# Where the last head pair's bonus step and its state store stand in a list of steps

## The chip, the cores and the metric

The kernel runs on one core of one Trainium2 chip. The metric is the device time of one execution in microseconds (us). The engines are TensorE (PE in the profile; its weight loads are PEld), VectorE (DVE), ScalarE (ACT), GpSimd (POOL) and SyncE (SP), which here only issues DMAs. Every engine works through its own instructions in order, and the engines hold each other by semaphores.

## The reference, cut to what matters

One layer of a hybrid model for 128 context tokens and 512 latent tokens, 1024 channels. Three branches read one input projection: an RWKV-7 scan of 8 heads of 64 channels in both directions, a gated MLP and a convolution. Their concatenation goes through one output projection; a mixture of 16 experts (top 2) follows. The part that the change touches is the scan branch:

```python
def step(s, inp):
    r_t, w_t, k_t, v_t, kk_t, a_t = inp
    s_kk = jnp.einsum('bhvk,bhk->bhv', s, kk_t)
    s = (s * w_t[:, :, None, :]
         - s_kk[..., None] * (kk_t * a_t)[:, :, None, :]
         + v_t[..., None] * k_t[:, :, None, :])
    return s, jnp.einsum('bhvk,bhk->bhv', s, r_t)
...
y = _head_norm(ys[0] + ys[1], lp['lnx_g'], lp['lnx_b'])
bonus = jnp.sum(heads(r) * heads(kts[0] + kts[1]) * lp['r_k'], axis=-1, keepdims=True) * heads(v)
ya = ((y + bonus.reshape(B, T, D_A)) * g).astype(h.dtype)
```

The kernel returns the outputs of both token groups and the scan's final context states (`new_state_rwkv`).

## The kernel before, in words

The work is done in stages: the modulation, the norm and the input projection with the gated MLP and the convolution; the scan; the output projection with the second norm and the router; the experts; the final norm. All five engines go from the scan to the output projection through `scan_done` (L1178), a list of semaphore waits on everything that the scan produced, among them `state_stored` (the state stores have landed) and `read_head_bonus` (the last head bonus is multiplied).

**The scan** works on four head pairs m = 0 to 3 (two heads, 128 partitions each). A pair's set-up is low_rank, decay, key_square, key_norm, mix, kk, factors and operands; `gram`, `keys`, `xloc`, `wqx`, `mr` work on one of five groups q of chunks (64 tokens each, both directions); diag, sub 1-30, turn, off, merge_a and merge_b invert the chunks' triangular matrices; `chain m s` carries the state through slot s (order 2, 0, 3, 1, 4 to 8; slots 0 and 1 are the context, so the final context state is there after `chain m 1`); `y m t` gives the output of one of five token tiles; `state_out` transposes the final context state, copies it and stores it; the head steps (head_stats, head_centre, head_scale, head_gain, head_bias, head_bonus) normalise the pair's output and add the bonus.

**The order is written out by hand.** `PLAN` (L338) is one text list of steps. `steps_of` turns it into `SCHEDULE`, and each of the engines walks the same list in its own function (`scan_loads` L498 for SyncE, `scan_pool` L536, `scan_act` L565, `scan_dve` L698, `scan_pe` L827) and issues its part of each step, with its waits. So a step's place in the list is its place in the queue of every engine that has a part in it.

**Shared PSUM.** Steps that write a temporary in PSUM take one of three double banks in turn, in the order of the list: `temp(st)` is `pp[i % 3]` for the i-th such step, and TensorE first waits until the step three places before has been read (`temp_free`, L394). bonus, state_out and head_bonus are among these steps; chain has its own banks.

**bonus m** has four parts: GpSimd adds the keys of both directions (L562, `kt_sum`), VectorE multiplies by r_k and r (L748, `bonus_terms`), TensorE sums over each head with five narrow matmuls (L864, `bonus_mm`), ScalarE copies the result (L619, `read_bonus`), which head_bonus reads. **state_out m**: four transposes on TensorE (L878) once `state_next (m, 1)` is up, a copy on ScalarE (L688) once the previous pair's store has landed, two DMAs of SyncE to the output (L532). **head_bonus m**: five transposes on TensorE (L883), a multiply (L491) and an add (L496) on VectorE.

**The early loads.** At the step `chain 3 2` SyncE reads back the two other branches into `catBC` and issues the loads for the next stage (`early_loads`, L1135: four DMAs, two of w_out and the two token groups). They overwrite buffers of the scan, so SyncE first waits for what still uses these:

```python
if st == ("chain", 3, 2):

    sp.wait_ge(*at("y_mm", (2, TILES_Y[-1])))
    sp.wait_ge(*at("keys_T", (3, STAGES[-1])))
    for n in ("factor", "end_factor", "operands_done", "bonus_mm", "excl", "kt_sum", "mb_mm", "read_merge_a", "wb_diag"):
        sp.wait_ge(*at(n))
    sp.wait_ge(*at("cat_moved", "stored"))
    sp.dma_start(catBC[:, :, :].rearrange("p c t -> p (c t)"), cat_dram).then_inc(*up16("cat_moved", "back"))
    early_loads(sp)
```

A name without a key stands for the semaphore's last count, that is all four pairs. SyncE's next step in the list is `state_out 3`, and behind that it goes on to the next stage (`post_loads`, L1184): the rest of w_out, the modulation rows, the norm's gain and the router's weights.

**Behind the scan** (`post_pe`, L1626, in the order of `ORDER`): TensorE's first work are the head matmuls (L1655, the gate), then the output projection's matmuls (L1647); VectorE's first is the gate's product (L1388).

Of the kernel before, what the change touches and what calls it, by code (L numbers as in the profile page):

```python
# [40 lines left out]
def build(nc, A, outs, counts):  # L41
# [25 lines left out]
    with ctx:  # L67
        counts.open(nc, ctx)

        def sb(name, shape, dt=F32):  # L70
            return ctx.enter_context(nc.sbuf_tensor(name, shape, dt))
# [219 lines left out]
        def ccols(c):  # L291
# [39 lines left out]
        bonus = sb("bonus", [P, NT, NH])  # L331
# [23 lines left out]
            keys 1 3 / sub 2 13 / mr 1 0 / wqx 1 2 / sub 2 14-15 / low_rank 3 1 1 / sub 2 16-17 / keys 1 4 / chain 1 0 / mr 1 2 /  # L355
            chain 1 3 / sub 2 18-19 / xloc 1 3 / chain 1 1 / wqx 1 3 / sub 2 20-22 / key_square 3 1 / chain 1 4 / xloc 1 4 / mr 1 3 /
            key_norm 3 0 / chain 1 5 / sub 2 23 / decay 3 1 / sub 2 24 / wqx 1 4 / state_out 1 / sub 2 25 / chain 1 6 / key_norm 3 1 /
            sub 2 26 / y 1 0 / mix 3 / mr 1 4 / sub 2 27 / chain 1 7 / sub 2 28 / factors 3 0 / head_scale 0 / sub 2 29 / y 1 2 /
            sub 2 30 / chain 1 8 / y 1 3 / turn 2 / off 2 / kk 3 0 / y 1 1 / factors 3 1 / kk 3 1 / operands 3 0 / merge_a 2 / y 1 4 /
            merge_b 2 / operands 3 1 / head_gain 0 / gram 2 1 / gram 2 0 / head_bias 0 / diag 3 / sub 3 1-3 / keys 2 1 / keys 2 0 /  # L360
            xloc 2 1 / head_bonus 0 / sub 3 4 / xloc 2 0 / gram 2 2 / gram 2 3 / wqx 2 1 / sub 3 5-6 / keys 2 2 / mr 2 1 / head_stats 1 /
            wqx 2 0 / init 2 / keys 2 3 / sub 3 7 / xloc 2 2 / sub 3 8 / chain 2 2 / xloc 2 3 / sub 3 9 / mr 2 0 / sub 3 10 / gram 2 4 /
            wqx 2 2 / chain 2 0 / chain 2 3 / sub 3 11-12 / mr 2 2 / keys 2 4 / chain 2 1 / sub 3 13-16 / wqx 2 3 / chain 2 4 / xloc 2 4 /
            mr 2 3 / wqx 2 4 / sub 3 17 / chain 2 5 / y 2 0 / sub 3 18-19 / chain 2 6 / sub 3 20 / mr 2 4 / sub 3 21 / chain 2 7 / y 2 2 /
            sub 3 22 / chain 2 8 / sub 3 23-25 / y 2 3 / sub 3 26 / y 2 1 / sub 3 27-28 / y 2 4 / sub 3 29 / state_out 2 / sub 3 30 /
            gram 3 1 / gram 3 0 / turn 3 / head_centre 1 / head_scale 1 / keys 3 1 / keys 3 0 / xloc 3 1 / off 3 / head_gain 1 / init 3 /
            gram 3 2 / merge_a 3 / head_bias 1 / head_bonus 1 / merge_b 3 / head_stats 2 / xloc 3 0 / gram 3 3 / wqx 3 1 / keys 3 2 /
            mr 3 1 / wqx 3 0 / xloc 3 2 / head_centre 2 / gram 3 4 / head_scale 2 / mr 3 0 / chain 3 2 / wqx 3 2 / keys 3 3 / chain 3 0 /
            keys 3 4 / xloc 3 3 / chain 3 3 / mr 3 2 / head_gain 2 / chain 3 1 / wqx 3 3 / chain 3 4 / y 3 0 / mr 3 3 / chain 3 5 /
            xloc 3 4 / head_bias 2 / chain 3 6 / wqx 3 4 / chain 3 7 / y 3 2 / mr 3 4 / y 3 3 / chain 3 8 / head_bonus 2 / y 3 1 / y 3 4 /  # L370
            bonus 3 / head_stats 3 / head_centre 3 / head_scale 3 / head_gain 3 / state_out 3 / head_bias 3 / head_bonus 3
        """


# [1850 lines left out]
```

## Time and profile before

| | |
|---|---|
| device time, median of 3 runs | 1016.51 us (1015.21 to 1020.67) |
| the profiled execution | 1015.5 us |
| its span | 1013.8 us, granted TensorE clock 0.876 on the mean |
| busy: PE, PEld | 795.3 us (78%), 494.0 us (49%) |
| busy: DVE, ACT, POOL | 499.8 us (49%), 264.2 us (26%), 127.9 us (13%) |
| moved by DMA | 150.58 MB |

The page gives shares over the whole span, which are means over stages with different limits. A stage is read from the timeline of each engine (what ran when, and in brackets how long the engine had been idle and what ended that) and from the list of waits. Busy times of TensorE rest on modelled ends of its matmuls.

### The profile page before, as it was taken

How to read it: one execution, taken by the hardware profiler on the slowest of the kernel's cores; microseconds unless marked ns; L12 is line 12 of the kernel's file. 1: busy time of each engine (PE TensorE's matmuls, PEld its weight loads, DVE VectorE, ACT ScalarE, POOL GpSimd, SP SyncE). 2: the span in 40 equal slices, each digit the busy share in tenths (PEclk: the TensorE clock that was granted, in tenths of full speed). 3: DMA queues.
4: the chain of work that ended last, by engine and by line, in shares of the span. 5: the costliest groups of instructions: out<-in, count | busy, mean ns of one | idle time of the engine just before them, and what ended most of it. 6: DMA issues, size and time to landing. Idle time of an engine off the chain costs nothing. (4 is left out here: it accounts for less than half of the span.)

```text
span 1013.8 us, 18006 instructions
## 1 busy us (share of the span) xinstructions
PE 795.3 (78%) x7510; PEld 494.0 (49%) x7510; DVE 499.8 (49%) x1052; ACT 264.2 (26%) x561; POOL 127.9 (13%) x127
## 2 busy tenths in 40 slices
PE   4589999999933719979699957998279999999800
PEld 3345455655522507767577743455244454444400
DVE  1210037575455898989999650533613333333302
ACT  2221013121246435646644610102010010000003
POOL 3000000000004130310300000000032222222050
PEclk9679999999966858979799978998569999999955
DMA  7952044064061000000000058101079999999476
GB/s 281 340 203 81 2 167 166 4 246 167 1 231 51 2 1 3 22 10 3 8 3 9 4 193 321 43 21 62 18 280 374 354 356 365 356 370 350 141 149 184
DMA packets 42442, 150.58 MB, mean 149 GB/s; under 512 B 6031, under 2 KB 8598, under 8 KB 37398
## 3 DMA queue, kind: packets, MB, share of 16 engines
q1 hardware_dynamic: 33142, 78.07, 21.4%
q0 software_dynamic: 9216, 71.31, 20.7%
q8 instruction: 62, 1.02, 0.4%
q14 instruction: 22, 0.18, 0.1%
HBM read 133.08 MB, written 22.05 MB: 153 GB/s over the span
## 5 line engine op out<-in xcount | busy, mean ns | idle before, releaser
L2167 PE MATMUL banks<-arena 128*128 128x512 f32 x304 | 157.4, 600 | 0.0
L1714 PE MATMUL banks<-arena 128*128 128x512 f32 x288 | 129.2, 602 | 1.1 <-ACT arena L1343 1.1
L2166 PEld LDWEIGHTS banks<-arena 128*128 128x128 f32 x304 | 57.9, 193 | 73.4 <-issue 71.5
L1714 PEld LDWEIGHTS banks<-arena 128*128 128x128 f32 x288 | 55.5, 193 | 71.1 <-issue 69.5
L1737 PE MATMUL banks<-arena 128*128 128x512 f32 x144 | 65.1, 595 | 1.6 <-DVEq L1160 1.6
L1586 DVE TENSOR_TENSOR arena<-arena,banks 128x256 f32<-128x256 f32 x18 | 7.6, 420 | 111.4 <-ACT arena L1349 105.5
L2046 DVE TENSOR_TENSOR arena<-arena 128x641 f32<-128x641 f32 x15 | 12.4, 827 | 99.6 <-ACT arena L1911 99.6
L2166 PE MATMUL banks<-arena 128*128 128x128 f32 x304 | 59.9, 279 | 1.5 <-ACT arena L201 1.5
L775 DVE TENSOR_TENSOR arena<-arena 128x30 f32<-128x30 f32 (+14 forms) x120 | 52.3, 436 | 4.1
L1349 ACT ACTIVATE arena<-banks 128x256 f32<-128x256 f32 x18 | 6.9, 385 | 180.5 <-PE banks L1714 180.5
L2036 DVE SCALAR_TENSOR_TENSOR arena<-arena 128x640 f32<-128x640 f32 x60 | 49.7, 878 | 0.0
L772 DVE TENSOR_TENSOR arena<-arena 128x30 f32<-128x30 f32 (+14 forms) x120 | 45.7, 381 | 2.7
L2167 PEld LDWEIGHTS banks<-arena 128*128 128x128 f32 x304 | 46.7, 194 | 0.0
L1260 POOL DMA_INDIRECT arena<-in_moe_w_gu_dram,loraT x18 | 17.1, 951 | 196.2 <-DVE arena L1553 115.4
L1601 DVE SCALAR_TENSOR_TENSOR arena<-banks,loraT,arena 128x512 f32<-128x512 f32 x36 | 25.4, 746 | 32.6 <-PE banks L1737 32.6
L1737 PEld LDWEIGHTS banks<-arena 128*128 128x128 f32 x144 | 26.1, 191 | 28.6 <-issue 25.8
L541 POOL MEMSET arena<- 128x2560 f32 x1 | 2.2, 2231 | 290.1 <-ACT catBC L211 290.1
L1647 PE MATMUL banks<-arena,catBC 128*128 128x512 f32 x80 | 36.3, 607 | 0.3 <-DVE rkvT L1398 0.3
L1647 PE MATMUL banks<-arena,rkvT 128*128 128x512 f32 x80 | 35.3, 593 | 0.0
L2150 PE MATMUL banks<-arena 128*128 128x512 f32 x80 | 34.5, 592 | 0.0
L1908 ACT ACTIVATE arena<-banks 128x128 f32<-128x128 f32 x15 | 4.2, 279 | 105.4 <-PE banks L2167 105.4
L259 PE MATMUL banks<-arena 128*2 128x128 f32 x768 | 26.5, 297 | 3.6 <-DMA arena<-in_ada_w_dram 3.6
(345 smaller groups left out, 1473.8 us busy)
## 6 DMA issues: line engine op xcount, KB each, us to landing
arena<-in_ada_w_dram SPq DMA_DIRECT2D x12, 2048.0 KB, 12.5
arena<-in_w_in_dram SPq DMA_DIRECT2D x5, 2048.0 KB, 14.9
slot_rows<-arena SPq DMA_DIRECT2D x18, 512.0 KB, 8.6
arena<-modulations SPq DMA_DIRECT2D x8, 512.0 KB, 8.2
h_rows<-arena SPq DMA_DIRECT2D x5, 512.0 KB, 2.6
out_dram<-arena SPq DMA_DIRECT2D x5, 512.0 KB, 4.1
arena<-in_x_sample_dram SPq DMA_DIRECT2D x4, 512.0 KB, 11.0
arena<-in_w_out_dram SPq DMA_DIRECT2D x1, 2048.0 KB, 10.6
```

What stands on the lines that cost most here:

```text
L259: x = nc.tensor.matmul(out[32 * g:32 * g + 2, :], silu_c[:, k, :], wslot(n)[:, k, g * P:(g + 1) * P], start=False, stop=(k == KD - 1), ski ...
L772: v.tensor_tensor(t, vsub[:, j + 1:32, j:j + 1].to_broadcast([P, n, j]), vsub[:, j:j + 1, 0:j].to_broadcast([P, n, j]), ALU.mult).then_inc ...
L775: v.tensor_tensor(vsub[:, j + 1:32, 0:j], vsub[:, j + 1:32, 0:j], t, ALU.add).then_inc(*up("inverse_step", ("sub_add", m, j)))
L1260: g.indirect_dma_start(wgu[:, s, :, :].rearrange("p k n -> p (k n)"), None, wgu_rows, bass.IndirectOffsetOnAxis(ap=weight_u[:, i:i + 1], a ...
L1601: v.scalar_tensor_tensor(yrow[:, i % 2, cs], ps[5 + hf][:, :], slot_gate[:, i:i + 1], gate_row[:, i % 2, cs], ALU.mult, ALU.mult) \
L1647: x = T_.matmul(ps[6 + hf][:, :], lhs, wout[:, i, hf * 512:(hf + 1) * 512], start=(i == 0), stop=(i == KD - 1))
L1714: x = T_.matmul(ps[2 + s][:, :], hT[:, s, c, :], wgu[:, s, c, :], start=(c == 0), stop=(c == KD - 1))
L1737: x = T_.matmul(ps[5 + hf][:, :], actT[:, s, c * P:(c + 1) * P], wdn[:, s, c, hf * 512:(hf + 1) * 512], start=(c == 0), stop=(c == 1))
L2036: v.scalar_tensor_tensor(dst, src, ccol[:, 2 * k + c:2 * k + c + 1], dst, ALU.mult, ALU.add) \
L2150: x = T_.matmul(ps[2 + t % 2][:, :], h1T[:, k, t * P:(t + 1) * P], wslot(n)[:, k, :], start=(k == 0), stop=(k == KD - 1))
L2166: T_.matmul(ctx_[:, 0:P], w, h1T[:, k, 0:P], start=(k == 0), stop=(k == KD - 1))
L2167: x = T_.matmul(lat[:, :], w, h1T[:, k, P:T], start=(k == 0), stop=(k == KD - 1))
```

## The change

Two steps of the list move. `bonus 3` stood behind `y 3 4`, the last output tile; now it stands behind `keys 3 4`, the last keys. `state_out 3` stood behind `head_gain 3`; now it stands behind `chain 3 8`, the last chain step, ahead of `head_bonus 2`. The rest of the text that differs is only wrapped differently. No instruction is added or taken away. The end of the list, before and after:

```diff
-            mr 3 1 / wqx 3 0 / xloc 3 2 / head_centre 2 / gram 3 4 / head_scale 2 / mr 3 0 / chain 3 2 / wqx 3 2 / keys 3 3 / chain 3 0 /
-            keys 3 4 / xloc 3 3 / chain 3 3 / mr 3 2 / head_gain 2 / chain 3 1 / wqx 3 3 / chain 3 4 / y 3 0 / mr 3 3 / chain 3 5 /
-            xloc 3 4 / head_bias 2 / chain 3 6 / wqx 3 4 / chain 3 7 / y 3 2 / mr 3 4 / y 3 3 / chain 3 8 / head_bonus 2 / y 3 1 / y 3 4 /
-            bonus 3 / head_stats 3 / head_centre 3 / head_scale 3 / head_gain 3 / state_out 3 / head_bias 3 / head_bonus 3
+            wqx 3 0 / xloc 3 2 / head_centre 2 / gram 3 4 / head_scale 2 / mr 3 0 / chain 3 2 / wqx 3 2 / keys 3 3 / chain 3 0 / keys 3 4 /
+            bonus 3 / xloc 3 3 / chain 3 3 / mr 3 2 / head_gain 2 / chain 3 1 / wqx 3 3 / chain 3 4 / y 3 0 / mr 3 3 / chain 3 5 /
+            xloc 3 4 / head_bias 2 / chain 3 6 / wqx 3 4 / chain 3 7 / y 3 2 / mr 3 4 / y 3 3 / chain 3 8 / state_out 3 / head_bonus 2 /
+            y 3 1 / y 3 4 / head_stats 3 / head_centre 3 / head_scale 3 / head_gain 3 / head_bias 3 / head_bonus 3
```

## Rows read from the trace of the kernel before

Times are us from the start of the span. The first group of a view says what its columns are.

**Rows 1.** the page: GB/s in 40 slices of the span

```profile
GB/s 281 340 203 81 2 167 166 4 246 167 1 231 51 2 1 3 22 10 3 8 3 9 4 193 321 43 21 62 18 280 374 354 356 365 356 370 350 141 149 184
```

**Rows 2.** list of waits, 560 to 725: waiter, releaser, us, times, longest

```profile
PE banks L1655 <- DMA out_dram<-arena: 18.1, 1, 18.1
...
POOL loraT L1234 <- DMA out_dram<-arena: 103.1, 1, 103.1
```

**Rows 3.** list of SyncE's own waits, whole span, same columns

```profile
SPq L524 <- PE banks L864: 41.0, 1, 41.0
```

**Rows 4.** timeline of SyncE's issues: start us, us, queue, line, operation

```profile
594.89 0.33 SPq L526 DMA_DIRECT2D catBC<-branches  x1
...
597.49 3.92 SPq L532 DMA_DIRECT2D out_dram<-arena  x2
...
614.13 0.39 SPq L1188 DMA_DIRECT2D arena<-in_w_out_dram  x1
```

**Rows 5.** DMA, 590 to 640: GB/s, 40 slices; an issue, KB, landing us

```profile
GB/s 0 7 13 0 123 205 401 398 416 426 423 406 410 416 416 410 403 381 68 0 82 308 406 423 419 423 416 209 341 298 397 419 416 397 134 3 13 0 0 0
...
out_dram<-arena SPq DMA_DIRECT2D x2, 32.0 KB, 14.7
```

**Rows 6.** the line of the state stores (L532), all eight

```profile
DMA to landing us min/median/max: 2.0/2.3/15.8
```

**Rows 7.** timeline of TensorE, 573 to 600: start us, us, line, operation, count

```profile
577.12 0.68 PE L920 MATMUL banks<-arena 64*64 64x64 f32 x16
...
593.25 1.30 PE L864 MATMUL banks<-head_select,arena 128*128 128x2 f32 x10 [0.58 <-DVE arena L748]
```

**Rows 8.** timeline of TensorE around an earlier bonus and an earlier state_out

```profile
393.79 1.28 PE L864 MATMUL banks<-head_select,arena 128*128 128x2 f32 x10
...
482.36 0.30 PE L878 MATMUL banks<-ident,arena 64*64 64x64 f32 x4
```

**Rows 9.** timeline of VectorE: [idle before, and what ended it]

```profile
578.61 0.29 DVE L823 TENSOR_TENSOR arena<-banks,arena 128x128 f32<-128x128 f32 x1 [2.68 <-PE banks L969]
...
592.23 0.88 DVE L748 SCALAR_TENSOR_TENSOR arena<-arena,param_cols,rkvT 128x640 f32<-128x640 f32 x1
...
598.68 0.82 DVE L491 TENSOR_TENSOR rkvT<-banks,bonus 128x640 f32<-128x640 f32 x1
```

**Rows 10.** timeline of ScalarE, 574 to 598

```profile
578.52 0.36 ACT L635 COPY arena<-banks 128x256 f32<-128x256 f32 x1
...
592.74 0.27 ACT L652 COPY arena<-banks 128x128 f32<-128x128 f32 x1 [0.82 <-PE banks L992]
```

**Rows 11.** windows: length, busy PE, PEld, DVE, ACT, POOL; PEclk, DMA share, GB/s

```profile
575.00:590.00 15.00, 15.00 (x398) 12.96 (x393) 5.92 (x19) 6.62 (x19) 0.00 (x0) 1.00 0.02 4
...
614.00:618.00 4.00, 3.71 (x5) 1.67 (x6) 0.69 (x1) 0.00 (x0) 1.51 (x11) 0.50 0.60 172
```

**Rows 12.** timeline of TensorE behind the scan, 600 to 730

```profile
614.29 2.05 PE L1655 MATMUL banks<-g,loraT 128*128 128x512 f32 x2 [18.13 <-DMA out_dram<-arena]
...
616.13 8.07 PE L1647 MATMUL banks<-arena,catBC 128*128 128x512 f32 x16
...
632.79 1.02 PE L1655 MATMUL banks<-g,loraT 128*128 128x512 f32 x2
...
650.07 7.03 PE L1647 MATMUL banks<-arena,catBC 128*128 128x512 f32 x16
```

**Rows 13.** windows of TensorE alone: busy us, granted clock, DMA share, GB/s

```profile
702.00:704.00 2.00, 0.82 (x6) 0.89 0.00 0
```

**Rows 14.** DMA, 10 to 60 (GB/s, queue q1); TensorE's timeline there

```profile
GB/s 297 382 390 385 388 387 387 385 388 387 388 385 392 379 388 387 387 400 405 381 363 193 194 244 220 205 301 392 388 397 390 398 385 383 387 392 393 377 385 378
...
q1 hardware_dynamic: 9345, 17.99, 103.3%
...
20.69 2.00 PE L259 MATMUL banks<-arena 128*2 128x128 f32 x64
```

**Rows 15.** DMA, 575 to 595, queue of instruction blocks: packets, MB, share

```profile
q8 instruction: 4, 0.07, 1.4%
```

More of the change, by code:

```diff
@@ L357, in build @@
             key_norm 3 0 / chain 1 5 / sub 2 23 / decay 3 1 / sub 2 24 / wqx 1 4 / state_out 1 / sub 2 25 / chain 1 6 / key_norm 3 1 /
-            sub 2 26 / y 1 0 / mix 3 / mr 1 4 / sub 2 27 / chain 1 7 / sub 2 28 / factors 3 0 / head_scale 0 / sub 2 29 / y 1 2 /
-            sub 2 30 / chain 1 8 / y 1 3 / turn 2 / off 2 / kk 3 0 / y 1 1 / factors 3 1 / kk 3 1 / operands 3 0 / merge_a 2 / y 1 4 /
-            merge_b 2 / operands 3 1 / head_gain 0 / gram 2 1 / gram 2 0 / head_bias 0 / diag 3 / sub 3 1-3 / keys 2 1 / keys 2 0 /
@@ L361, in build @@
[L361 to L364, printed above, removed]
@@ L365, in build @@
-            sub 3 22 / chain 2 8 / sub 3 23-25 / y 2 3 / sub 3 26 / y 2 1 / sub 3 27-28 / y 2 4 / sub 3 29 / state_out 2 / sub 3 30 /
-            gram 3 1 / gram 3 0 / turn 3 / head_centre 1 / head_scale 1 / keys 3 1 / keys 3 0 / xloc 3 1 / off 3 / head_gain 1 / init 3 /
-            gram 3 2 / merge_a 3 / head_bias 1 / head_bonus 1 / merge_b 3 / head_stats 2 / xloc 3 0 / gram 3 3 / wqx 3 1 / keys 3 2 /
-            mr 3 1 / wqx 3 0 / xloc 3 2 / head_centre 2 / gram 3 4 / head_scale 2 / mr 3 0 / chain 3 2 / wqx 3 2 / keys 3 3 / chain 3 0 /
@@ L369, in build @@
-            keys 3 4 / xloc 3 3 / chain 3 3 / mr 3 2 / head_gain 2 / chain 3 1 / wqx 3 3 / chain 3 4 / y 3 0 / mr 3 3 / chain 3 5 /
-            xloc 3 4 / head_bias 2 / chain 3 6 / wqx 3 4 / chain 3 7 / y 3 2 / mr 3 4 / y 3 3 / chain 3 8 / head_bonus 2 / y 3 1 / y 3 4 /
-            bonus 3 / head_stats 3 / head_centre 3 / head_scale 3 / head_gain 3 / state_out 3 / head_bias 3 / head_bonus 3
+            sub 2 26 / y 1 0 / mix 3 / mr 1 4 / sub 2 27 / chain 1 7 / sub 2 28 / factors 3 0 / head_scale 0 / sub 2 29 / y 1 2 / sub 2 30 /
@@ new lines, in build @@
+            chain 1 8 / y 1 3 / turn 2 / off 2 / kk 3 0 / y 1 1 / factors 3 1 / kk 3 1 / operands 3 0 / merge_a 2 / y 1 4 / merge_b 2 /
+            operands 3 1 / head_gain 0 / gram 2 1 / gram 2 0 / head_bias 0 / diag 3 / sub 3 1-3 / keys 2 1 / keys 2 0 / xloc 2 1 /
+            head_bonus 0 / sub 3 4 / xloc 2 0 / gram 2 2 / gram 2 3 / wqx 2 1 / sub 3 5-6 / keys 2 2 / mr 2 1 / head_stats 1 / wqx 2 0 /
+            init 2 / keys 2 3 / sub 3 7 / xloc 2 2 / sub 3 8 / chain 2 2 / xloc 2 3 / sub 3 9 / mr 2 0 / sub 3 10 / gram 2 4 / wqx 2 2 /
@@ new lines, in build @@
+            chain 2 0 / chain 2 3 / sub 3 11-12 / mr 2 2 / keys 2 4 / chain 2 1 / sub 3 13-16 / wqx 2 3 / chain 2 4 / xloc 2 4 / mr 2 3 /
+            wqx 2 4 / sub 3 17 / chain 2 5 / y 2 0 / sub 3 18-19 / chain 2 6 / sub 3 20 / mr 2 4 / sub 3 21 / chain 2 7 / y 2 2 / sub 3 22 /
+            chain 2 8 / sub 3 23-25 / y 2 3 / sub 3 26 / y 2 1 / sub 3 27-28 / y 2 4 / sub 3 29 / state_out 2 / sub 3 30 / gram 3 1 /
+            gram 3 0 / turn 3 / head_centre 1 / head_scale 1 / keys 3 1 / keys 3 0 / xloc 3 1 / off 3 / head_gain 1 / init 3 / gram 3 2 /
@@ new lines, in build @@
+            merge_a 3 / head_bias 1 / head_bonus 1 / merge_b 3 / head_stats 2 / xloc 3 0 / gram 3 3 / wqx 3 1 / keys 3 2 / mr 3 1 /
+            wqx 3 0 / xloc 3 2 / head_centre 2 / gram 3 4 / head_scale 2 / mr 3 0 / chain 3 2 / wqx 3 2 / keys 3 3 / chain 3 0 / keys 3 4 /
+            bonus 3 / xloc 3 3 / chain 3 3 / mr 3 2 / head_gain 2 / chain 3 1 / wqx 3 3 / chain 3 4 / y 3 0 / mr 3 3 / chain 3 5 /
+            xloc 3 4 / head_bias 2 / chain 3 6 / wqx 3 4 / chain 3 7 / y 3 2 / mr 3 4 / y 3 3 / chain 3 8 / state_out 3 / head_bonus 2 /
```

## The prediction

> **What bounds the kernel now.** I began with the page: the span is the 1013.8 us of the table above, and the kernel runs through stages one after the other, so what a change in one stage is worth has to be read there. The list of waits over the end of the scan and the start of the stage behind it has one entry that dwarfs the others: TensorE's first matmul behind the scan (L1655) sat 18.1 us until a DMA from the arena to an output, the state store, had landed [rows 2]. Next come SyncE's own waits: at L524 its queue stood 41.0 us until the bonus matmuls (L864) were done [rows 3]. L524 is the first of the five early loads' chain of waits that had not yet come; the wait on `bonus_mm` asks for the count of all four pairs, and the last is pair 3. SyncE's timeline puts it in order [rows 4]: the five loads are issued from 594.89 on, the state store of pair 3 goes out behind them on the same queue from 597.49 on, and 614.13 is when SyncE, held by the same `scan_done`, goes on. The rate of the DMA engines shows what filled the time: fifteen slices of 1.25 us, nearly all of them at 380 to 426 GB/s, some 6.6 MB in all, and the store lands about 14.7 us after its issue [rows 5]. The eight state stores have a median of 2.3 us and a longest of 15.8 us [rows 6]: the last pair alone is slow, and it is the one behind the loads. VectorE finished the scan's work, the head bonus of pair 3, at about 600.4 (the multiply from 598.68 to 599.50, then one add) [rows 9]. So between 600.4 and 614.3 nothing computes; a 64 KB store waits out 6.6 MB of loads, and the loads waited for five narrow matmuls at 593.25 [rows 7].
>
> **What the change does to this, part by part.** *Bonus 3 behind keys 3 4.* What is removed at the tail is a VectorE product (0.88 us), a group of ten TensorE passes (1.30 us) and a ScalarE copy; their removal there frees nothing, because the last `y` copy ends at 593.01 [rows 10], when the product was just ending (592.23 + 0.88) [rows 9], and the head statistics need that copy in any case. What is added: the same three in the middle of the chain. VectorE: 0.88 us in a stretch where it sat 2.68 us for TensorE [rows 9], so nothing. GpSimd's sum for it needs no other step of the chain: GpSimd did nothing for the 103.1 us before 614.3 [rows 2], so it was made by 511; a late sum would hold TensorE's queue and all its chain steps. ScalarE: one short copy between the `keys 3 4` copies, the last of them ending at 578.88 [rows 10], and a copy that waits for TensorE; nothing. TensorE: it was busy in 15.00 of 15.00 us from 575 to 590 [rows 11], the other engines wait for it, so here I charge the step in full: 1.28 us, as another bonus step cost in a dense stretch [rows 8]. Above would be a stall on the way in, below zero by hidden latency; 0 to 2 us.
>
> The shared PSUM buffers rotate by three, so a step put into the list makes the three steps behind it wait for readers one place later in the list. For `xloc 3 3` that is the copy of `keys 3 3`, over before it; for `mr 3 2` that of `keys 3 4`, over at 578.88 [rows 10], while TensorE in its new timing can't reach it before 579.4 (577.12, the bonus at 1.28, `xloc` and `chain`) [rows 7, 8]; the third waits for the bonus copy itself. None adds.
>
> *State_out 3 behind chain 3 8.* Four small transposes, 0.30 us [rows 8], on a TensorE that has no idle time there; charged in full. ScalarE's copy leaves its place behind the head statistics and comes at about 591.5. `y 3 4` now waits for that copy, and can't start before 593 anyhow. The store itself, two DMAs, is issued at about 591.7 instead of 597.49.
>
> *The five loads*, not named in the diff, are what moves. TensorE reaches the bonus at 577.12, where `xloc 3 3` now starts [rows 7]; it ends at 578.40. Before, SyncE issued 0.34 us behind the modelled end (593.25 + 1.30 to 594.89) [rows 4, 7], so now at 578.74. The other waits of that list are for work of pair 3's set-up and for `keys 3 4`, all done by then. From the first load to the landed store it was 614.13 - 594.89 = 19.24 us [rows 4]; the same again gives 597.98 for the state store, if it queues behind all the loads as before.
>
> *The end of the scan.* VectorE's tail comes 1.28 + 0.30 = 1.58 us later: the head bonus multiply, the last thing that `scan_done` wants of VectorE, ends at 599.50 + 1.58 = 601.08. That is 3.1 us later than the store, so the tail now ends last. With the 0.16 us between SyncE's and TensorE's release before [rows 4, 12], TensorE starts again at 601.2 instead of 614.29: **13.1 us** earlier. What follows starts from the same `scan_done` on every engine, with the same queue behind it, and is shifted whole: the first reader of the loads finds them landed, as before.
>
> *The clock.* Behind the pause before, the granted clock was at 0.50, the lower of its two levels (1.2 GHz) [rows 11]: the pair of head matmuls took 2.05 us where a later one took 1.02, the first sixteen of the output projection 8.07 where a later group took 7.03 [rows 12]. Those 2.1 us would be saved if the shorter pause, about 6 us (from the last `y` copy's start, 592.74 + 1.58 [rows 10], and five transposes of the head bonus, to 601.2), kept the clock up. I don't count on it: at 702 to 704, with TensorE busy for only 0.82 of 2 us, the granted clock's mean had already fallen to 0.89 [rows 13]. TensorE: Matmul & The Clock Gate, in the Trainium skill (Why this matters for your kernels), warns of a slower clock after idle gaps between bursts of matmuls; by that rule too the 2.1 us are paid again.
>
> Sum: 1015.5 us for the profiled execution (1013.8 of span and 1.7 around it) less 13.1 gives **1002.4 us**. That execution lies 1.0 below the median of the three runs shown (1016.51), which the same step would take to 1003.4; both lie in what follows.
>
> **The rivals.** *More is gained* (17%): TensorE takes the two moved steps in the shadow of waits that the modelled matmul ends hide (1.58 us), or the clock stays up (2.1 us). Both give 998.7, one alone 1000.3 to 1000.8. For it: the profile's matmul ends are modelled, so that 15.00 of 15.00 may hide short waits. Against: those 15.00 as they stand, and the clock's row.
>
> *The store still ends last* (13%): the loads now run beside the scan's last steps, and if they are slower, the store lands later than 601.1. The 3.1 us of slack are gone when the loads' 15.9 us (6.6 MB at some 415 GB/s) become 19, at 347 GB/s; at the 281 GB/s of the page's first slice [rows 1] they take 23.5 us, the store lands at 605.6 and the time is 1007. Against: 380 to 400 GB/s beside a working TensorE at 10 to 60 us [rows 14].
>
> *The loads are not released* (5%): another wait of SyncE's list, or the place of the loads in the queue, keeps them where they are. Then the store at 591.7 isn't ahead of them, since SyncE's order has the loads first; the pause stays, the moved steps come on top, and the time is 1015 to 1017: no change. Against: the wait that ended last is named, L864 [rows 3].
>
> *Slower than before* (3%): TensorE's instructions come by DMA, through the same engines as the loads; four such blocks came in 575 to 595 [rows 15]. If each stood behind the loads as the state store did (14.7 us instead of 2.3, [rows 5, 6]), 12.4 us each, TensorE would stand still in the scan's last steps. It decides from a total of 13.1 us, that is with two blocks of the four late and not fetched ahead; two are 24.8 us, 1027 us. Against it: at 20.69, with the DMA queue at 103% of the 16 engines' time over 10 to 60, TensorE issued 64 narrow passes in 2.00 us without idling [rows 14]. The Trainium skill has both halves: Runtime: NRT & Kernel Launch (Instruction fetch mechanics) says that instructions are fetched by DMA ahead of use, and DMA: Bandwidth & Descriptors (Queues, rings and completion order) that a DMA engine takes turns between queues packet by packet; by the second, a block would not wait out the loads and this rival would cost almost nothing. No row here shows the turn-taking itself.
>
> **How the numbers follow.** The forecast, with 62%, is 1002.4. The range takes in the larger gain (998.7) and most of the later store, with the 1.0 us to the median: 998.5 to 1006.5. Runs of this kernel can tell about 0.5% from no change, 5.1 us. Below 1011.4 are the forecast, the larger gain and the later store: 92% faster; 5% the same; 3% slower.
>
> **What would show it.** In the profile after, SyncE's loads should be issued at 578 to 580, the state store at 591 to 593, with a landing time of some 5 to 6 us; TensorE's first L1655 should stand at about 601 with an idle time of about 6 us before it, ended by VectorE's head bonus (L491), not by a DMA; `xloc 3 3` and all behind it should stand 1.2 to 1.6 us later, with the same spacing. If the idle time before L1655 is ended by a DMA, the store still ends last; if gaps open in TensorE's scan steps under the loads, they are slowed by them; if the loads start later than 581, I have read the wait wrongly.

## The result and the profile after

The changed kernel takes 1011.99 us (median of 15 runs, 1008.6 to 1014.77), the kernel before beside it 1016.69 us (15 runs, 1014.96 to 1021.18). The ratio, which goes by the means of all runs (1011.7 and 1017.9 us) and not by the medians, is 0.994, 95% interval 0.9923 to 0.9957: 6.1 us less (4.4 to 7.8). The forecast was 1002.4 us, 13.1 us less; the range ended at 1006.5 us. The direction was right, and less than half of the gain came.

The profiled execution of the changed kernel took 1014.77 us, the longest of its fifteen. SyncE's timeline in it, columns as in [rows 4]:

```profile
584.28 0.33 SPq L526 DMA_DIRECT2D catBC<-branches  x1
...
602.14 1.31 SPq L532 DMA_DIRECT2D out_dram<-arena  x2
```

The loads go out 10.6 us earlier than before, and the state store no longer stands behind them. It lands within 2.9 us; the line of the state stores, which answers to [rows 6]:

```profile
DMA to landing us min/median/max: 2.0/2.2/2.9
```

TensorE's list of waits, 560 to 725, columns as in [rows 2]:

```profile
PE banks L1655 <- issue: 7.4, 1, 7.4
PE banks L878 <- issue: 3.2, 1, 3.2
...
PE banks L969 <- issue: 1.3, 1, 1.3
```

The 18.1 us for the store's landing are gone. In their place stand 7.4 us put down to "issue", time in which the profile shows nothing that the engine waited for, and two entries that are not in the list of before at all: 3.2 us at a state_out transpose (L878) and 1.3 us at a chain step (L969). TensorE's timeline shows where, columns as in [rows 7]:

```profile
582.67 1.28 PE L864 MATMUL banks<-head_select,arena 128*128 128x2 f32 x10
...
594.17 0.45 PE L969 MATMUL banks<-arena 64*64 64x64 f32 x8 [1.33 <-issue]
...
597.97 0.30 PE L878 MATMUL banks<-ident,arena 64*64 64x64 f32 x3
...
601.47 0.24 PE L878 MATMUL banks<-ident,arena 64*64 64x64 f32 x1 [3.20 <-issue]
...
602.36 1.18 PE L984 MATMUL banks<-arena 128*64 128x64 f32 x16
603.47 0.71 PE L992 MATMUL banks<-arena 64*64 64x64 f32 x16
604.10 1.17 PE L984 MATMUL banks<-arena 128*64 128x64 f32 x16
...
613.99 2.05 PE L1655 MATMUL banks<-g,loraT 128*128 128x512 f32 x2 [7.43 <-issue]
615.83 8.77 PE L1647 MATMUL banks<-arena,catBC 128*128 128x512 f32 x16
```

The longer wait lies between the third and the fourth of four transposes, and the fourth needs nothing that the third did not. Behind it the `y` steps (L984) take 1.17 us; in the kernel before they took 0.70:

```profile
591.58 0.70 PE L984 MATMUL banks<-arena 128*64 128x64 f32 x16
592.21 0.46 PE L992 MATMUL banks<-arena 64*64 64x64 f32 x16
```

VectorE's head bonus of pair 3 then ends at 612.69, columns as in [rows 9]:

```profile
611.87 0.82 DVE L491 TENSOR_TENSOR rkvT<-banks,bonus 128x640 f32<-128x640 f32 x1
```

**One measure for all runs.** In this execution bonus 3 starts at 582.67, 5.5 us later than `xloc 3 3`, whose place it takes, did in [rows 7]. That difference arose ahead of the moved steps and comes and goes between executions of one kernel (the last section). So from here on I read the stretch from bonus 3's start to the first L1655 (L1654, L1659 or L1660 in kernels with other line numbers), the **restart**. The forecast has 601.2 - 577.12 = 24.1 us for it; the changed kernel has 613.99 - 582.67 = 31.3. Of the missing 7.2 us, 6.1 lie ahead of the end of the multiply (612.69 - 582.67 = 30.0 instead of 601.08 - 577.12 = 24.0) and 1.1 between it and the restart (1.30 instead of 0.16).

### The profile page after: what moved, and what is told of

Same layout as the page of the kernel before. It is cut to its first block and busy times, and to the rows that moved or that the text cites. A ratio compares the mean times of both kernels' runs of the same rounds, so it can differ in the third digit from the quotient of the medians.

```text
span 1013.0 us, 18006 instructions
## 1 busy us (share of the span) xinstructions
PE 801.1 (79%) x7510; PEld 499.7 (49%) x7510; DVE 500.2 (49%) x1052; ACT 264.2 (26%) x561; POOL 128.1 (13%) x127
## 5 line engine op out<-in xcount | busy, mean ns | idle before, releaser
L2046 DVE TENSOR_TENSOR arena<-arena 128x641 f32<-128x641 f32 x15 | 12.4, 827 | 99.6 <-ACT arena L1911 99.6
L802 DVE TENSOR_TENSOR arena<-banks,causal_mask 128x512 f32<-128x512 f32 x40 | 25.4, 683 | 7.8 <-PE banks L896 7.7
```

The source lines that it names most:

```text
L802: v.tensor_tensor(dst, t[:, :, :, w, :], gmask[:, w, :, :, :].rearrange("p i d n -> p (i d) n").unsqueeze(1).to_broadcast([P, 2, 4, 64]), ...
```

## The experiments

**The theories.** *A*: TensorE's instructions arrive by DMA in blocks, and beside the loads these come late, so that it runs out of instructions. The page counts 62 such blocks on queue q8 in the whole execution, and on TensorE 7510 matmuls and 7510 weight loads, by far the most of any engine, which makes some 242 instructions a block:

```profile
q8 instruction: 62, 1.02, 0.4%
```

Narrow windows of the DMA view of the changed kernel speak for it: 584 to 591, 591 to 593, 593 to 598 and 598 to 600 (queue: packets, MB, share of 16 engines' time):

```profile
q1 hardware_dynamic: 321, 2.04, 79.4%
...
q1 hardware_dynamic: 198, 0.81, 100.0%
q8 instruction: 1, 0.02, 3.0%
...
q1 hardware_dynamic: 548, 2.05, 102.0%
...
q1 hardware_dynamic: 196, 0.80, 99.6%
q8 instruction: 1, 0.02, 3.3%
```

In the first and the third window no block came. Windows of 0.1 us put the blocks at 577.1, 583.9, 591.8, 598.9 and 603.4; in the kernel before they came at 578.2, 582.8, 587.3 and 592.5. Gaps of 4.5 to 5.2 us became 7.9 and 7.1 under the loads, and both waits of TensorE end 2.3 to 2.5 us behind the window in which a late block is transferred. From the end of the one wait to the end of the other TensorE ran 124 matmuls and 123 weight loads, about one block (columns as in [rows 11]):

```profile
594.17:601.47 7.30, 4.10 (x124) 3.43 (x123) 1.40 (x5) 0.53 (x2) 0.00 (x0) 1.00 1.03 410
```

The kernel before has two such waits too, earlier in the scan, where no load runs at all:

```profile
391.59 0.65 PE L934 MATMUL banks<-arena 64*64 64x128 f32 x7 [1.32 <-issue]
...
514.00 0.45 PE L909 MATMUL banks<-ident,arena 128*64 128x128 f32 x4 [0.84 <-issue]
```

Blocks came at 389.0 and 511.6, so these two end 2.4 to 2.5 us behind a block as well. Ahead of the first, TensorE had run 163 matmuls and 144 weight loads from 388 to 390. So it can run out of instructions without any load beside it. (Two more issue waits of the scan, 4.21 us at 304.12 and 0.48 us at 427.49, have no block right ahead of them, and no run explains them.)

The other theories. *B*: the moved state_out causes the wait that lies in it. *C*: one unlucky execution. *D*: loads kept out of the scan cost as much behind it.

**The changed kernel again.**

> The changed kernel once more, nothing edited, for a second profile. Theory A (the loads, now beside the scan's last steps, hold up the blocks of instructions that TensorE fetches by DMA): waits of 1 to 4 us that end with no releaser (issue) stand again in TensorE's scan steps between the first load and the last, at the same instructions, and not ahead of the loads; time 4 to 6 us below the kernel before. Rival B (the moved steps themselves wait): the waits stand at the bonus and state_out steps alone. Rival C (one unlucky execution): no such waits in this profile, and the time is 10 us or more below the kernel before.

1010.19 us; ratio 0.9922 (0.9895 to 0.9948). The waits are at the same instructions, TensorE's timeline:

```profile
593.04 0.45 PE L969 MATMUL banks<-arena 64*64 64x64 f32 x8 [1.07 <-issue]
600.34 0.29 PE L878 MATMUL banks<-ident,arena 64*64 64x64 f32 x1 [3.20 <-issue]
612.92 2.04 PE L1655 MATMUL banks<-g,loraT 128*128 128x512 f32 x2 [7.43 <-issue]
```

C falls. The waits belong to a place in the instructions, again 124 matmuls and 123 weight loads apart. Bonus 3 starts at 581.80: 31.1 us to the restart.

**Each part alone.** The first kernel moves only bonus 3, the second only state_out 3:

```diff
 (bonus alone, against the changed kernel)
-... / chain 3 8 / state_out 3 / head_bonus 2 / ... / head_gain 3 / head_bias 3 / ...
+... / chain 3 8 / head_bonus 2 / ... / head_gain 3 / state_out 3 / head_bias 3 / ...
 (state_out alone, against the kernel before)
-... / chain 3 8 / head_bonus 2 / ... / head_gain 3 / state_out 3 / head_bias 3 / ...
+... / chain 3 8 / state_out 3 / head_bonus 2 / ... / head_gain 3 / head_bias 3 / ...
```

> Only bonus 3 is moved; state_out 3 stands behind head_gain 3 as before. Theory A: the loads start where they do in the changed kernel, so the waits without a releaser are there again in the scan's last steps, one of them no longer inside the four transposes of state_out but in whatever step follows there; the store is issued some 3 us before the last head bonus multiply and lands about 2.5 us later with the loads done, so the time is within 2 us of the changed kernel. Rival B: the 3.2 us inside state_out's transposes go away with the step, and the time is 3 us or more below the changed kernel.

1012.74 us; ratio 0.9928 (0.9899 to 0.9958). TensorE's timeline:

```profile
583.83 1.28 PE L864 MATMUL banks<-head_select,arena 128*128 128x2 f32 x10
595.04 0.45 PE L969 MATMUL banks<-arena 64*64 64x64 f32 x8 [1.06 <-issue]
601.42 0.38 PE L883 MATMUL banks<-ident,rkvT 128*128 128x128 f32 x2 [2.02 <-issue]
612.17 2.05 PE L1655 MATMUL banks<-g,loraT 128*128 128x512 f32 x2 [7.19 <-issue]
```

The second wait is still there with no state_out in its place: it has gone into the transposes of head_bonus 2, a few instructions from where it was and still 124 matmuls behind the first wait. B falls, and bonus 3 alone brings the whole gain that can be measured. In this profile the restart comes 28.3 us behind bonus 3, 3.0 less than in the changed kernel: the two waits are 1.45 us shorter, and the `y` steps behind them take 0.70 us, as before the change. The time of the whole does not show these 3 us.

> Only state_out 3 is moved; bonus 3 stands behind y 3 4 as before. Theory A: the loads start behind the late bonus as before, no wait without a releaser stands in the scan's last steps, the store still queues behind the loads, and the time is that of the kernel before, within 2 us. Rival B: the wait of some 3 us inside state_out's transposes is there without any loads beside it, and the time is 2 to 4 us above the kernel before.

1018.45 us; ratio 0.9997 (0.9972 to 1.0022): nothing. The transposes run without a wait, since the loads are out only at 595.92, and the store still lands last:

```profile
590.62 0.30 PE L878 MATMUL banks<-ident,arena 64*64 64x64 f32 x4
...
615.35 2.04 PE L1655 MATMUL banks<-g,loraT 128*128 128x512 f32 x2 [19.15 <-DMA out_dram<-arena]
```

**The loads behind the store.** The block of SyncE's waits and loads stands behind pair 3's state store in place of `chain 3 2`:

```diff
-                if st == ("chain", 3, 2):
+                if st == ("state_out", 3):      # and below the store
                     sp.wait_ge(*at("y_mm", (2, TILES_Y[-1])))
```

> Both steps moved as in the changed kernel, but SyncE issues the read-back and the four loads behind the state store of pair 3 instead of at chain 3 2, so nothing but that store moves beside the scan's last steps until about the last two y steps. Theory A: no wait without a releaser up to there, the last head bonus multiply ends 5 to 6 us sooner after the bonus step than in the changed kernel, the store lands about 2.5 us after its issue; the loads then run beside VectorE's tail and land 9 to 16 us after it, so that the first output projection matmuls may wait 0 to 2 us for w_out; time 1003 to 1007. Rival B: the wait inside state_out stays, time within 2 us of the changed kernel. Rival D (the loads are needed that early): TensorE waits 5 us or more for w_out or the read-back behind the scan and the time is no lower than that of the changed kernel.

1017.11 us; ratio 0.9978 (0.9953 to 1.0004). TensorE's timeline:

```profile
577.96 1.28 PE L863 MATMUL banks<-head_select,arena 128*128 128x2 f32 x10
...
603.08 2.05 PE L1654 MATMUL banks<-g,loraT 128*128 128x512 f32 x2 [7.44 <-issue]
613.36 6.88 PE L1646 MATMUL banks<-arena,catBC 128*128 128x512 f32 x9 [8.24 <-DMA arena<-in_x_sample_dram]
```

No issue wait from bonus 3 to the end of the scan, and the multiply ends 601.78 - 577.96 = 23.8 us behind bonus 3's start: the forecast's 24.0, once nothing is loaded beside the scan. The steps from bonus 3 on are those of the changed kernel in the same order, and their blocks come at 578.8, 584.5, 589.1 and 593.4: gaps of 5.7, 4.6 and 4.3 us, where the loads had made 7.9 and 7.1 of the first two. But the projection waits 8.24 us for the loads, so D holds too, and of the gain nothing that these runs can tell is left.

**The weights earlier, the rest behind the store.** Everything of the weights' buffer is free already when pair 3 starts. So w_out's two loads go behind pair 3's state load, and `catBC` and the token groups behind the state store, the latter on a semaphore of their own:

```diff
+                    if m == 3:                  # at gram 3 1
+                        sp.wait_ge(*at("y_mm", (2, TILES_Y[-1])))
+                        early_weights(sp)       # the two loads of w_out
...
-                if st == ("chain", 3, 2):
+                if st == ("state_out", 3):      # and below the store
...
+            sp.dma_start(x1[:, 0, :], A["x_prompt"][0]).then_inc(*up16("x1_landed"))
```

> Both steps moved, and each load put where its own buffer is free and where it meets little of TensorE's dense stretch: the two w_out loads (2.5 MB) go out behind the state load of pair 3, once pair 2's last output tile is done; the read-back and the two x1 loads go out behind the state store of pair 3, and x1 has a semaphore of its own, so that TensorE and SyncE wait for w_out alone. Theory A: no wait without a releaser between keys 3 4 and y 3 4; one or two of 1 to 3 us beside the w_out loads, in a stretch where TensorE waits for VectorE as well; TensorE starts behind the scan about 25 us after the bonus step (in the changed kernel 31), finds w_out there, and doesn't wait for x1; time 8 to 12 us below the kernel before. Rival E (a byte loaded beside the scan costs the same wherever it is put): time no lower than that of the changed kernel, 5 to 8 us below the kernel before.

1010.57 us; ratio 0.9917 (0.9894 to 0.9939). TensorE's timeline:

```profile
566.07 0.26 PE L1038 MATMUL banks<-arena 32*32 32x32 f32 x1 [2.58 <-issue]
586.41 1.28 PE L866 MATMUL banks<-head_select,arena 128*128 128x2 f32 x10
611.53 2.04 PE L1660 MATMUL banks<-g,loraT 128*128 128x512 f32 x2 [7.43 <-issue]
```

The wait has moved with the loads: w_out is issued at 557.6, and the wait is now in pair 3's merges. The restart comes 25.1 us behind bonus 3 (the changed kernel: 31.3), but the wait of 2.58 us now lies ahead of bonus 3, outside this measure. The ratio is not to be told from those of the changed kernel (0.994 and 0.9922), so the time alone does not refute the rival named in the expectation.

**The lag of the release.** `scan_done` has 27 waits; the one that comes true last, `read_head_bonus`, has ten behind it. Here it stands last:

```diff
-            for n in ("y_mm", ..., "state_next", "state_stored", ..., "wb_diag", "read_head_bonus", ..., "turned", "mb_mm"):
+            for n in ("y_mm", ..., "state_next", ..., "wb_diag", ..., "turned", "mb_mm", "state_stored", "read_head_bonus"):
```

> The changed kernel with the list in scan_done in another order: state_stored and read_head_bonus, the two that come last, at its end, instead of with 22 and 10 waits behind them. If the 1.3 us between the end of the last head bonus multiply and TensorE's first matmul in the changed kernel is time in which the engines work through waits that are long fulfilled, it falls to 0.3 to 0.6 us, and SyncE's and GpSimd's starts move alike; time 0.5 to 1.2 us below the changed kernel, which is about what three rounds can just not tell. If it is the way of one semaphore, it stays at 1.1 to 1.5 us.

1014.04 us; ratio 0.9953 (0.9932 to 0.9973). The multiply ends at 613.55, and TensorE's timeline has

```profile
613.70 2.05 PE L1655 MATMUL banks<-g,loraT 128*128 128x512 f32 x2 [6.01 <-DVE rkvT L491]
```

The lag is 0.15 us instead of 1.30, less than I had expected (0.3 to 0.6), so it was the working through of waits that had long come true. The later kernels agree: 0.14 to 0.15 us in the five profiles with this order of the list, 1.30 in three runs above with the old one (bonus alone, the loads behind the store, the weights earlier). The issue waits stand at the same two instructions again, 1.21 and 2.65 us. The profile now names the releaser, where it had said "issue". What this is worth in the whole time, these runs don't resolve.

**A load in the kernel before.** The order of steps is that of before; SyncE only copies twice 2 MB between DRAM buffers beside pair 2's chain, work added for the test:

```diff
+                if st == ("chain", 2, 2):
+                    sp.wait_ge(*at("chain_mm", (2, 2)))
+                    for i in range(2):
+                        sp.dma_start(y_dram[512 * i:512 * i + 512, :], A["x_sample"][0]).then_inc(*up16("slots_cleared"))
```

> The kernel before, its list untouched, with two copies of the latent tokens (2 MB each) from one DRAM tensor to rows of another that are written over later, issued beside pair 2's chain, where nothing else is loaded. They change no result. Theory A: TensorE, which has no wait without a releaser there in the kernel before, gets one or two of 1 to 4 us between 528 and 550, some 256 instructions apart or a multiple of that; time 1 to 5 us above the kernel before, less where VectorE's work covers the wait. Rival B (the waits belong to the moved steps): none, and the time within 1 us of the kernel before.

1023.9 us; ratio 1.0055 (1.0027 to 1.0083), some 5.6 us slower. The copies go out at 528.82. TensorE's timeline:

```profile
535.79 0.32 PE L912 MATMUL banks<-ident,rkvT 128*64 128x128 f32 x1 [0.98 <-issue]
545.32 0.69 PE L938 MATMUL banks<-arena 64*64 64x128 f32 x4 [4.27 <-issue]
```

Neither wait is in the trace of before, where blocks came at 529.7, 534.2 and 539.7; here they come at 533.2 and 543.0, and the waits end 2.3 to 2.5 us behind them. From the one to the other it is 124 matmuls and 124 weight loads, the same stretch as in the changed kernel:

```profile
535.79:545.32 9.53, 5.00 (x124) 4.34 (x124) 5.21 (x16) 2.87 (x8) 0.00 (x0) 0.90 0.65 215
```

The two waits add up to 5.25 us, about what the kernel lost. No step of the list was moved: bulk transfers beside TensorE's work are enough to make it wait for instructions. That is A shown as far as the trace goes.

**Both repairs.** The weights earlier and the last of the waits last:

> The kernel with each load put by its region, and the order of scan_done's list changed as in the run on that order. Both by theory A and by the account of the waits: 0.5 to 1.2 us below the kernel with the loads by region alone, 9 to 13 us below the kernel before. If the two don't add up, the time is that of the loads by region alone.

> The version with the weights' loads back to back behind pair 3's state load and scan_done's order changed, once more, on the same chip as the loads in pieces. One issue wait of about 2 us at the merge step (L1038), the restart 24.1 us behind the bonus step of pair 3, 1006.5 to 1011 us.

1008.24 us; ratio 0.9902 (0.9881 to 0.9923); again, on another chip, 1007.39 us, 0.9893 (0.9866 to 0.9920). The first one's timeline of TensorE:

```profile
562.44 0.26 PE L1038 MATMUL banks<-arena 32*32 32x32 f32 x1 [2.03 <-issue]
582.42 1.28 PE L866 MATMUL banks<-head_select,arena 128*128 128x2 f32 x10
606.52 2.04 PE L1660 MATMUL banks<-g,loraT 128*128 128x512 f32 x2 [6.28 <-DVE rkvT L491]
```

Bonus 3 to restart: 24.1 us, the forecast's figure to the tenth; in the second 24.0. One wait of 2.03 us is left in the merges in both, ahead of bonus 3. The gain over the weights earlier alone (0.9917), expected at 0.5 to 1.2 us, is within the noise of these ratios.

**The weights in pieces.** Against the last kernel, w_out's 2.5 MB come as five loads of 512 KB, each behind one of pair 3's chain steps 0 to 4, and, to tell spacing from place, as the same five all behind `chain 3 2`:

```diff
 (spaced)
+                if st[0] == "chain" and st[1] == 3 and st[2] < 5:
+                    sp.wait_ge(*at("chain_mm", st[1:]))
+                    early_weights(sp, st[2])    # 512 KB
 (at once)
+                if st == ("chain", 3, 2):
+                    sp.wait_ge(*at("chain_mm", st[1:]))
+                    for i in range(5):
+                        early_weights(sp, i)
```

> The best version so far (weights apart from the rest, scan_done's order changed), but with the 2.5 MB of the output projection's weights as five loads of 512 KB, each issued only when one of pair 3's chain steps 0 to 4 is done, in place of two loads back to back. The rest is loaded behind the state store, as there. If an instruction block is late because it stands behind what is already queued, a burst of 512 KB (about 1.3 us at 400 GB/s) can hold it by about that much, less than TensorE has in hand: issue waits under 0.5 us in the scan (2.03 us there), none right behind a piece; the bonus step of pair 3 at 577 to 580, TensorE's restart 24.1 us behind it; 1003 to 1006 us. If it is the bytes moved beside the scan, whatever their spacing, that cost TensorE, the waits add up to 1.5 to 2.5 us as there and the time is 1007 to 1010. If the last piece lands behind the restart, the first matmul of the projection waits for it, which the trace would name.

1003.94 us (1002.03 to 1013.64); ratio 0.9893 (0.9851 to 0.9935). On this chip the kernel without pieces has the same ratio (0.9893, the second run above), so a gain from the pieces in the whole time is not shown. From 560 to the restart TensorE's timeline has no issue wait at all:

```profile
578.04 1.28 PE L866 MATMUL banks<-head_select,arena 128*128 128x2 f32 x10
...
602.00 2.05 PE L1659 MATMUL banks<-g,loraT 128*128 128x512 f32 x2 [6.28 <-DVE rkvT L491]
```

> The version with the five loads spaced by chain steps, once more, on the same chip as the five at once: no issue wait of TensorE from 560 to the restart, which comes 24.0 us behind the bonus step of pair 3; 1002 to 1005 us in most runs.

1007.28 us (1002.99 to 1009.66); ratio 0.9867 (0.9837 to 0.9897). One issue wait of 0.18 us, where none was expected; 24.5 us from bonus 3 to the restart. Two of the six runs lie within the 1002 to 1005 us expected of most.

> The version with five loads of 512 KB, but all five issued together when the first of pair 3's chain steps (chain 3 2) is done, at 573.8 by the trace of the spaced version: the same bytes, the same start, no spacing. The backlog is then 2.5 MB, about 6.3 us at 400 GB/s, over some 574 to 581. If the backlog is what holds an instruction block up, TensorE has an issue wait of 1 to 2.5 us within 576 to 584, with steps at half clock behind it, and the restart comes 2 to 5 us later than with the spaced loads: 1006 to 1009 us. If it is the place in the scan that mattered (the merges of pair 3 against its chain), there is no issue wait and the time is the spaced version's, 1003 to 1005.

1006.7 us (1003.76 to 1009.41); ratio 0.9865 (0.9836 to 0.9893), not to be told from the spaced loads beside it (0.9867). The time lies in the range that I had given for a wait from the backlog of 2.5 MB, but the spaced loads took as long on this chip, and the trace has no such wait. TensorE's timeline, and the DMA view of 579 to 587:

```profile
583.60 1.28 PE L867 MATMUL banks<-head_select,arena 128*128 128x2 f32 x10
607.90 2.05 PE L1660 MATMUL banks<-g,loraT 128*128 128x512 f32 x2 [6.28 <-DVE rkvT L491]
```

```profile
q1 hardware_dynamic: 642, 2.37, 82.1%
```

Queue q8 has no row in it: here no block came between 578.0 and 587.0, a longer gap than those of the changed kernel, and TensorE did not run dry. In the spaced version, too, it takes blocks only every 5.5 to 7.3 us at this place (567.0, 572.5, 579.6 and 585.3; in the second profile 570.1, 577.4 and 584.3), against gaps of 3.7 and 6.5 us in the merges of before (556.5, 560.2 and 566.7), where the same bytes back to back cost 2.0 to 2.6 us. So the spacing was not needed. What is left is that 2.5 MB, not 6.6, were loaded, and that loading began some 6 us earlier, measured against bonus 3 (4.2 us ahead of its start instead of 1.6 behind it). These runs don't separate how much of it is the bytes and how much the place.

## Why the prediction missed, point by point

**The mechanism of the gain was right.** Bonus 3 started in the place of `xloc 3 3`, without a wait, in 1.28 us, and the loads followed it as forecast: 584.28 is 578.74 and the 5.54 us by which this execution was late. The store went out at 602.14 (591.7, 5.54 of lateness and 4.53 of the two waits make 601.8) and landed in 2.7 us. The tail, not the store, ends last. State_out's move alone brings nothing, which the prediction did not say: it gave the two moves one sum.

**The step that failed is that the loads beside the scan cost nothing.** They were moved from a pause into a stretch where TensorE was busy in 15.00 of 15.00 us [rows 11], and there is no term for it in the sum. The rows had the cause: four blocks of instructions in 20 us [rows 15]. I made it a rival with an all-or-nothing price, 12.4 us a block, that decided from two blocks, and gave it 3%. I did not look for waits of this kind in the trace of before, which has two (1.32 us at 391.59, 0.84 us at 514.00) with no load beside them: it showed that TensorE was close to running out of instructions as it was. What came was the mechanism at a smaller price, 1.33 and 3.20 us: the sign of the change stayed, its size did not. Behind the second wait the granted clock fell to 0.78 on the mean of 600 to 604, and the `y` steps took 0.95 us (L984, twice) and 0.44 us (L992) longer than at full speed. In all 4.53 + 1.39 = 5.9 of the 6.1 us that the multiply was late.

**The counter-evidence was too weak for its use.** The 64 narrow passes at 20.69 without idling [rows 14] took 2.00 us, and no block was due: in the first 60 us q8 brought blocks at 25.5 and 33.5 alone, so those passes say nothing of a block beside loads. Of the Trainium skill, DMA: Bandwidth & Descriptors (Queues, rings and completion order) lets the DMA engines take turns between queues packet by packet. The runs bear that out in part: the blocks of 591.8 and 598.9 landed in windows in which the loads had 100% of the engines' time, so they did not wait out the loads. But they came late, and the cost was not nearly nothing, as the prediction had it by that rule. Of the Trainium skill, Runtime: NRT & Kernel Launch (Instruction fetch mechanics) calls the cost of crossing from one block to the next mostly hidden. The trace agrees for the scan's last 30 us before the change (no issue wait there); beside the loads the cost was not hidden, nor was it at 391.59 and 514.00 of the kernel before, with the DMA engines idle.

**Two terms were mis-sized.** The release lag was taken as 0.16 us from a row where SyncE and TensorE were let go by the same store, which is no measure of the waits still to be worked through; it was 1.30. And the price of the low clock was put at 2.1 us again; the first sixteen matmuls of the projection took 8.77 us (8.38 in the second profile) instead of 8.07 [rows 12], 0.7 us more. The shorter pause did not keep the clock up: the row of 614 to 618 has 0.50 again, as in [rows 11]. The windows of the changed kernel, columns as there:

```profile
600.00:604.00 4.00, 2.53 (x38) 2.15 (x38) 1.44 (x2) 0.36 (x1) 0.00 (x0) 0.78 0.62 230
...
614.00:618.00 4.00, 4.00 (x5) 1.81 (x6) 0.69 (x1) 0.00 (x0) 1.23 (x10) 0.50 0.87 255
```

So the larger gain's clock did not come either. Nor did its other half, the two steps in the shadow of hidden waits: with no load beside the scan the multiply ended 23.8 us behind bonus 3's start, where 24.0 charges both steps in full and 22.4 (599.50 - 577.12) neither. With the sizes of the one profile, the sum would have been 13.1 less 6.1, 1.1 and 0.7, which is 5.2 us; measured over all runs were 6.1 (4.4 to 7.8).

**The range** had an end for a slower load (1006.5 to 1007) and none for the loads slowing TensorE; one block at that rival's own price (1002.4 and 12.4) would have reached beyond the result. With fewer bytes loaded beside the scan, at another place, and `scan_done` in order, the three runs with the weights in pieces came 10.9 to 13.8 us below the kernel before, at ratios of 0.9893, 0.9867 and 0.9865, where the forecast is 0.987. These kernels are not the one that was forecast, so this agreement does not make the forecast right.

## What to carry to other kernels

When an early release pulls bulk loads beside an engine that is full of small instructions, charge the loads to that engine: count how often its instruction blocks come in the trace, and look for "issue" waits in the middle of work that waits for nothing, in the kernel before too. Of what is loaded early, only what the next stage reads first needs to be early, at a place where the trace then shows no such wait, and the rest can go behind the last store. In a long list of waits the one that comes true last belongs at the end.

## What the runs showed of the hardware

Late instruction blocks cost waits at the same instructions in each of three profiles (1.33, 1.07 and 1.21 us; 3.20, 3.20 and 2.65 us), not at random ones. Such waits, of 0.8 us and more, ended 2.3 to 2.5 us behind the transfer of a block, beside loads and without them, and two in a row lay 124 matmuls and 123 or 124 weight loads apart. About ten waits that had come true took 1.15 us to work through (1.30 against 0.15). Where the delay of a block arises, in the DMA engines' queues or on the way from memory, no run told apart.

Executions of one kernel differ by 5 us ahead of the moved steps, with TensorE's clock. The two profiles of the kernel with spaced loads, in windows of TensorE alone (columns as in [rows 13]):

```profile
560.00:570.00 10.00, 8.67 (x253) 1.00 0.01 3
```

```profile
560.00:570.00 10.00, 8.44 (x215) 0.75 0.01 3
```

Bonus 3 starts at 578.04 in the one and at 583.06 in the other, and the spans are 1000.3 and 1006.6 us. These two come from different chips, but one chip alone gave six runs of this kernel between 1002.03 and 1013.64 us. The profiled execution of before was one with 1.00 at 560 to 570, that of the changed kernel one with 0.74. Two profiles of single executions would have shown 0.8 us between the kernels (spans of 1013.8 and 1013.0), where the medians show 4.7.
